# Moving a 3 MB weight load, the convolution's taps and its diagonals in the second layer of a hybrid diffusion backbone

## The reference

```python
q, k, v, u = jnp.split(h_lat @ w_in, cuts, axis=-1)      # one input projection of 1792 columns
q = apply_rope(rmsnorm(split_heads(q, N_HEADS), q_g), cos, sin)
k = apply_rope(rmsnorm(split_heads(k, N_KV_HEADS), k_g), cos, sin)
a_lat = blocked_gqa(q, k_all, v_all)                     # 8 query heads, 2 key heads of 64
c_lat = conformer_conv(u, w_dw, b_dw, ln_g, ln_b)        # GLU, depthwise conv of 31 taps, LayerNorm, silu
o_lat = jnp.concatenate([a_lat, c_lat], axis=-1) @ w_out
x = x + g1 * o_lat
# layer 0: dense SwiGLU (2816 wide); layer 1: the two best of 8 experts
f_lat = swiglu(h_lat, ffn_w1[i], ffn_w3[i], ffn_w2[i])
```

## Time and profile before

| | |
|---|---|
| time, median of 3 runs | 1595.78 us (1593.43 to 1595.98) |
| profiled execution | 1595.78 us, span 1593.6 us |
| TensorE busy | 96% of the span |
| VectorE, ScalarE busy | 70%, 57% |
| mean granted clock of TensorE | 0.981 |

### The profile page before, as it was taken

How to read it: one execution, slowest core, us unless ns; L and a number is a source line. 1 busy time by engine, 2 the same in 40 slices (tenths; PEclk the granted TensorE clock), 3 DMA queues, 4 the chain that set the end, 5 groups by cost and what they waited for, 6 DMA issues and landing times.

```text
span 1593.6 us, 21238 instructions
## 1 busy us (share of the span) xinstructions
PE 1523.1 (96%) x8897; PEld 1252.6 (79%) x8897; DVE 1123.4 (70%) x1202; ACT 908.8 (57%) x991; POOL 7.8 (0%) x8
## 2 busy tenths in 40 slices
PE   6899889999999999897899999999999999999997
PEld 3788558788888888884877888888888888888885
DVE  2899864422323234788578897898979898888996
ACT  3422673422223224755676777777777777777774
POOL 0000000000000000000000000000000000000100
PEclk8999899999999999998999999999999999999999
DMA  9979613532221425104349999999999999999991
GB/s 354 384 269 353 228 54 99 166 106 94 72 72 53 165 100 171 67 1 159 133 162 322 373 385 330 373 388 374 377 334 378 383 370 360 355 382 380 373 392 70
DMA packets 195414, 396.89 MB, mean 249 GB/s; under 512 B 6992, under 2 KB 54640, under 8 KB 195312
## 3 DMA queue, kind: packets, MB, share of 16 engines
q1 hardware_dynamic: 192896, 388.82, 67.8%
q10 hardware_dynamic: 1840, 4.55, 0.8%
q0 software_dynamic: 576, 2.10, 0.3%
HBM read 390.72 MB, written 4.72 MB: 248 GB/s over the span
## 4 chain that ended last, share of the span: by engine, by line
PE 89%; DVE 4%; DMA 3%; ACT 1%; issue 1%; SPq 1%; DVEq 0%; ACTq 0%
PE bank L1106 10%; PE bank L1108 10%; PE bank L1107 10%; PE bank L1135 5%; PE bank L1137 5%; PE bank L1136 5%; PE bank L963 5%; PE bank L962 5%; PE bank L961 5%; PE bank L697 4%; PE bank L698 4%; PE bank L699 4%; DMA weight_ring<-in_w_ada 3%; PE bank L970 2%; PE bank L972 2%; PE bank L971 2%
## 5 line engine op out<-in xcount | busy, mean ns | idle before, releaser
L1690 DVE TENSOR_TENSOR unit_lo_halves<-weight_ring,unit_hi_halves 128x2048 fp32r<-128x2048 f32 x264 | 594.2, 2285 | 30.7 <-ACT unit_hi_halves L1336 29.9
L1336 ACT ACTIVATE unit_hi_halves<-weight_ring 128x2048 fp32r<-128x2048 f32 x264 | 506.5, 1919 | 158.0 <-PE bank L1108 85.5
L1106 PE MATMUL bank<-unit_hi_halves,gathered_halves 128*128 128x512 f32 (+1 forms) x768 | 289.7, 377 | 0.0
L1108 PE MATMUL bank<-unit_lo_halves,gathered_halves 128*128 128x512 f32 (+1 forms) x768 | 285.6, 372 | 0.0
L1107 PE MATMUL bank<-unit_hi_halves,gathered_halves 128*128 128x512 f32 (+1 forms) x768 | 285.4, 372 | 0.0
L1108 PEld LDWEIGHTS bank<-unit_lo_halves,gathered_halves 128*128 128x128 f32 x768 | 144.6, 188 | 25.7
L1107 PEld LDWEIGHTS bank<-unit_hi_halves,gathered_halves 128*128 128x128 f32 x768 | 144.9, 189 | 23.4
L1106 PEld LDWEIGHTS bank<-unit_hi_halves,gathered_halves 128*128 128x128 f32 x768 | 144.7, 188 | 23.2
L1135 PE MATMUL bank<-unit_hi_halves,scratch_halves 128*128 128x512 f32 x352 | 137.6, 391 | 0.9 <-DVE scratch_halves L2124 0.9
L1137 PE MATMUL bank<-unit_lo_halves,scratch_halves 128*128 128x512 f32 x352 | 137.2, 390 | 0.0
L1136 PE MATMUL bank<-unit_hi_halves,scratch_halves 128*128 128x512 f32 x352 | 137.1, 390 | 0.0
(11 more groups left out here) (294 smaller groups left out, 2117.4 us busy)
## 6 DMA issues: line engine op xcount, KB each, us to landing
weight_ring<-in_exp_w SPq DMA_DIRECT2D x264, 1024.0 KB, 6.2
weight_ring<-in_w_ada SPq DMA_DIRECT2D x24, 2048.0 KB, 13.8
weight_ring<-in_ffn_w SPq DMA_DIRECT2D x33, 1024.0 KB, 5.3
weight_ring<-in_w_in SPq DMA_DIRECT2D x8, 1024.0 KB, 11.5
weight_ring<-in_w_out SPq DMA_DIRECT2D x4, 2048.0 KB, 10.9
weight_ring<-in_w_in SPq DMA_DIRECT2D x2, 3072.0 KB, 15.3
expert_rows<-scratch ACTq DMA_DIRECT2D x7, 512.0 KB, 5.3
hT<-in_x SPq DMA_DIRECT2D x1, 1024.0 KB, 5.4
```

Source lines behind the costliest of these rows:

```text
L1106: mm(ps, xg_hi[place(e)][:, k, :], hi[:, q, :], start=(k == 0), stop=False)
L1108: i = mm(ps, xg_hi[place(e)][:, k, :], lo[:, q, :], start=False, stop=(k == KT - 1))
L1336: f(hi_unit(v), raw_unit(v), ACT.Copy).then_inc(unit_hi, 1)
L1690: tt(lo_unit(v), raw_unit(v), hi_unit(v).bitcast(F32), ALU.subtract).then_inc(unit_lo, 1)
```

## The change

It moves work in four places and adds none but, perhaps, where a table is loaded.

1. The load `heads(1)` goes from before the fifth `w2` load to behind `units(1, 1)`. Tiles 0 to 4 of layer 1 are prepared one product row earlier on ScalarE and VectorE.
2. ScalarE: diagonals 12 to 16 come before tile 10; at c == 3 tiles 11 and 12 come before the diagonals 17 to 27.
3. `root_table(7)` is dropped.
4. VectorE: at c == 3 only 2 taps; the remainders of tiles 11 to 13 go to st = 0, 1 and 2, where they come first; 7 taps in each st (before 2, 4, 5, 5, 5, 7); 4 taps in each of the pair steps 0 and 1 (before 2 in step 1). The wait before L1867 follows the count.

```diff
-            if g == 4:
-                heads(1, STAGE)
...
         units(1, 0, 2)
         units(1, 1, 3)
+        heads(1, STAGE)
         out_projection(1, 0, 0)
...
                         mixer_halves(1, 9)
                         tap_of_bias(2)
+                        conv_diagonals(12, 17)
                         mixer_halves(1, 10)
-                        conv_diagonals(12, 17)
                     elif c == 3:
                         tap_of_bias(3)
-                        conv_diagonals(17, 20)
-                        root_table(7)
                         mixer_halves(1, 11)
-                        conv_diagonals(20, 28)
                         mixer_halves(1, 12)
+                        conv_diagonals(17, 28)
...
-                        if n in (19, 20):
-                            mixer_halves(1, 2 * n - 38)
-                            mixer_halves(1, 2 * n - 37)
-                        if n == 21:
+                        if n in (18, 19):
+                            mixer_halves(1, 2 * n - 36)
+                            mixer_halves(1, 2 * n - 35)
+                        if n == 20:
                             mixer_halves(1, 4)
...
                     elif c == 3:
-                        conv_steps(4)
-                        mixer_rest(1, 11)
-                        conv_steps(6)
-                        mixer_rest(1, 12)
-                        conv_steps(12)
+                        conv_steps(2)
...
-                    if l == 0 and st < 3:
-                        mixer_rest(0, V_TILE + 3 + st)
+                    if st < 3:
+                        mixer_rest(l, V_TILE + 3 + st)
...
-                    if l == 1 and st == 1:
-                        mixer_rest(1, IN_TILES - 1)
...
-                    conv_steps([2, 4, 5, 5, 5, 7][st] if l else TAPS_AT_HEAD[st])
+                    conv_steps(7 if l else TAPS_AT_HEAD[st])
...
-                    dve.wait_ge(m["conv_step"], 76)
+                    dve.wait_ge(m["conv_step"], 72)
...
-                    if l == 1 and st == 1:
-                        conv_steps(2)
+                    if l == 1 and st < 2:
+                        conv_steps(4)
```

More of the change, by code:

```diff
@@ L331, in backbone @@
                             (f_mm, 4 * g + 4), g % STAGE) for g in range(NF // 2)]
-        F[0]["w2"] = []
-        for g in range(NF // 2):
-            if g == 4:
-                heads(1, STAGE)
-            F[0]["w2"].append(fill([(2, D, 0, t["ffn_w2"][0][256 * g:256 * g + 256, :]
-                                     .rearrange("(k p) n -> p k n", p=P))],
-                                   (y_part, 2 * g + 2) if g < NF // 2 - 1 else (y_mm, KT), (NF // 2 + g) % STAGE))
+        F[0]["w2"] = [fill([(2, D, 0, t["ffn_w2"][0][256 * g:256 * g + 256, :]
+                             .rearrange("(k p) n -> p k n", p=P))],
+                           (y_part, 2 * g + 2) if g < NF // 2 - 1 else (y_mm, KT),
+                           (NF // 2 + g) % STAGE) for g in range(NF // 2)]
         units(1, 0, 2)
         units(1, 1, 3)
+        heads(1, STAGE)
         out_projection(1, 0, 0)
@@ L1965, in _ @@
                         second_rest(n)
[L1966 to L1969, removed]
+                        if n in (18, 19):
+                            mixer_rest(1, 2 * n - 36)
+                            mixer_rest(1, 2 * n - 35)
+                        if n == 20:
                             mixer_rest(1, 4)
```

## The result

The changed kernel took 1614.05 us by the median of four runs (1608.21 to 1615.93), beside 1595.88 us for the kernel before; the ratio is 1.011, with a 95% interval of 1.0081 to 1.0139. Run once more beside the kernel before on another occasion it took 1608.45 us against 1595.01, a ratio of 1.008 (1.006 to 1.010). The forecast of 1610.9 us is a ratio of 1.0095 and lies in both intervals. The change makes the kernel about 1% slower, clear of noise. Taken together, the eight runs of the changed kernel behind these two medians have a median of 1611.2 us. The changed kernel scatters by 6 to 8 us from run to run, the kernel before by 3 to 8.

The account below looks back on a forecast made before the run. TensorE, busy 96% of the span, was taken as the bound, so time is lost only where it waits. Terms 5.5 + 1.9 + 1.9 + 1.7 + 1.1 + 3.0 = 15.1 us on 1595.8 gave 1610.9 us, range 1603.5 to 1614.5.

Parts of the forecast that it names:

- Rival B: At the diagonal gap in layer 1's mixer the clock holds: 1610.9 - 1.7 = 1609.2 us; chance 20%.
- rival D: More half clock among the first score pairs, or a table switch 1.4 us dearer: 1612.3 to 1613 us; chance 12%.
- Rival C: Among the first score pairs the extra taps hide, with TensorE at half clock: 1607.9 us; chance 10%.
- Rival E: Fewer taps ahead of L1867 remove TensorE's 3.0 us wait: 1592.8 us, if the load's stall is absent too; chance 2%.

Follow-up runs that it names:

- part 1 alone: The kernel before with only the 3 MB load behind units(1, 1) and tiles 0 to 4 one row earlier: 1604.56 us against 1594.67, ratio 1.006.
- parts 2, 3 and 4 alone: Each part by itself in the kernel before: part 2 (preload kept ahead of the two tiles) 1599.72 us, part 3 1598.21, part 4 1597.75, each against 1594.67.

## Why the prediction was right, and where it was off

**Part 1** was right in mechanism and a little small. The wait was put at 5.8 us and is 6.8, and the last row starts 6.5 us later where 5.5 stood, since the load took 15.2 us from its issue, where 14.3 had been worked out. (That working has a slip of its own: 628.2 + 7.7 is 635.9, not 636.1.) Two experiments show that it takes both the late load and the copy's place. The clock behind it was put at 1.9 us; by the profiles it is 1.35 (part 1 alone), 2.0 and 2.9 (the changed kernel).

**Part 2** was right to 0.1 us: 1.9 for the copies and 1.6 for the clock, where 1.9 and 1.7 stood. Rival B, the clock holding, did not come about in any of the three profiles with this gap.

**Part 3**: 1.20 us, where 1.1 stood. The price of 2.66 us in the Trainium skill (ScalarE: Activation LUTs, "What ACT_TABLE_LOAD costs") does not hold here, and with it that half of rival D is out.

**Part 4** was right: VectorE's work up to L1867 grew by 0.05 us (0.3 worked out, nothing taken), the six more taps cost 3.35 us where 3.0 stood; 0.3 of it is a gap of VectorE's ahead of `rope(4)`, which lies between. One sign was off: VectorE waited 12.2 us for the root, where some 9 stood. That costs nothing by itself, since the reciprocal starts with the root either way. Rival C is out: the first value products give back only 0.2 and 0.65 us in the changed kernel. The other half of rival D came about in the clock: it is at half speed for 13.7 us among the first pairs in all four profiles with part 4 in them (10.2 before). No step behind the first normalisation is longer for it, though it may be why rival C's slack gave so little back; no run separates the two. Rival E was tried from the other end: fewer taps ahead of L1867 do bring it forward by 3.1 us, but at the cost of the pairs.

**What the sum left out** is the stretch after the product. At layer 1's first norm the kernel before is at half clock from 648 to 655, 6.8 us; the changed kernel's first profile has 10.2 there, which cost 1.5 us. It is not an effect of the change that can be shown: the same 10.2 us stand in the profiles of parts 2, 3 and 4 alone, whose code before that place is the old one, and 6.8 us in the other profiles of the changed order.

The sum of the four steps is 16.5 to 17.6 us in the profiles, 15.1 in the forecast; the two comparisons give 13.4 and 18.2. The scatter of several microseconds leaves open which is nearer. The range ends at 1614.5 us, so the first median of 1614.05 is only just inside it; the second, and the 1611.2 of all eight runs, lie well inside. The sum did not come out by errors that cancel: every term is within 1 us of what it measured. The second median alone would fit rival B (1609.2) or C (1607.9) as well; what speaks against them is the rows.

## What to carry to other kernels

A late load costs little by itself. What decides is the first instruction that waits for it, and what stands behind that instruction on an in-order engine: here the same late landing cost 0.7 us (within the noise) with the copy last and 7.5 to 9.9 us with the copy ahead of the last row's halves.

Work that an engine has to do anyway is free only in the time in which it waits. Moving taps behind the bound gained nothing; moving them ahead, into waits of 2 us each, gained 2.2 us, and with the diagonals 5.4.

## What I had not expected of the hardware

The same gap of TensorE's does not always bring the lower clock. At the end of the mixer TensorE waits 1.65 us before L668 in every one of the thirteen profiles, with the same work ahead of it. Behind it the clock was at half speed for 3.4 us in the kernel before and stayed up in the run with the diagonals early:

```profile
765.00:767.00 2.00, 0.54 (x10) 0.29 (x6) 0.90 (x2) 1.94 (x5) 0.00 (x0) 1.00 0.00 0
767.00:768.00 1.00, 0.81 (x5) 0.72 (x6) 0.74 (x4) 1.00 (x1) 0.00 (x0) 1.00 0.00 0
768.00:771.00 3.00, 3.00 (x26) 3.00 (x26) 2.17 (x6) 2.62 (x7) 0.00 (x0) 1.00 0.00 0
```

The stretch of 3.4 us was there in five of the thirteen profiles, absent in the other eight, and is worth 1.5 us. The stretch at the start of layer 1 held 10.2 us at half clock in four profiles and 6.8 us in the other nine. Gaps of 3.0 us and more at the diagonals brought half clock in all four profiles that have one, the gap of 1.1 us in none. So an effect of 1 to 2 us is better read from the steps in the profile, one place to the next, than from the time of few runs.
